# Weighted sum of gathered rows: four products of 256 columns in four column strips, and x1, y and the final norm held as feature quarter by token

## The chip, the cores and the metric

One core of a Trainium2 chip runs the program; all data is fp32. The metric is the device time of one execution in microseconds (us), lower is better.

## The reference

One layer of a decoder trunk for 1,088 tokens (1,024 of a prompt, 64 samples), model width 1,024. A mixer (projections, a recurrent group, a short convolution, attention into memory) and a layer norm give x1; after it comes PEER, a retrieval of single-neuron experts, and the second layer norm. The change lies in these last two:

```
x = LN1(alpha*x + mixer(x))                 # x1
q = x @ wq                                  # 8 heads, 2 keys each, 128 x 128 = 16384 experts
e, s = top 16 of each head                  # 128 experts a token
g = softmax(s)
act = gelu(sum_d x[t,d] * u[e[t,h,k], d])
f[t] = sum_{h,k} g[t,h,k] * act[t,h,k] * v[e[t,h,k]]
y = LN2(alpha*x + f)                        # mean and variance over the 1024 features
```

## The kernel before

The mixer runs in three blocks of tokens (384, 384, 320). PEER runs in tiles of 128 tokens (`TILES` = 8, and a ninth tile of 64), each tile in 128 **slots** (the ninth in 64), 1,088 slots in all. A slot n takes 32 tokens of the tile (a *place* `c`, four in a tile, two in the ninth), one head and a quarter `m` of the 16 experts of each token: 128 rows of the table `uv`, one on each partition, four for each of the 32 tokens. A row is 8 KB, its u half and its v half. In a slot:

- POOL (line 685) gathers the 128 rows with one indirect DMA into buffer n mod 8 of `ring`. It first waits for `used` to reach n-7, which is the weighted sum of slot n-8, the last reader of that buffer.
- PE `replicate` (L961) has spread x1 of the 32 tokens over the 128 partitions by a product with a 0/1 matrix `sel` (32 rows deep), and ACT (L1167) copied it to SBUF as `xrep`; this is done once for a group of two or four slots, 176 times in all, one group ahead.
- DVE (L1618) takes the dot product of row and `xrep`, 128x1024.
- ACT makes gelu (L1188), times the gate (L1192), and `wset` (L1197), a 128x32 matrix that holds each row's weight in its token's column.
- PE `combine(n)` (L979) multiplies `wset` with the v half and adds it up in PSUM (`ps`, two banks of 128x512, called `ybank`): two products of 512 columns. The output has 32 rows only, so each product takes a strip of 32 of the array's 128 columns. `quad(t, c)` gives the two strips: feature half 0 of place c goes to strip c, feature half 1 to strip (c+2) mod 4. It then raises `used`.

So y of a tile lies as two feature halves in the free direction, the second with its partitions turned by 64; `x1b` (x1 of the tile, later y, two buffers) lies the same way, which takes three loads (`load_x1`, L566) and three stores (`store_y`, L579) a tile on SP's queue. On DVE, `residual` (L1556, part 0 after half of a tile's slots, part 1 eight slots into the next tile) adds alpha*x1 to the sum; `finish` (L1565) takes the norm's statistics per half (`bn_stats`), swaps them between partition halves by small copies, and applies the norm; its statistics run 21 slots into the next tile (`FINISH`), in one piece between two dots. After the last slot residual and finish run at once, and SP stores the last tile.

Each engine has its own instruction stream, in an order fixed when the program is built: the slot loop, and between the slots steps of the mixer and of the queries from a plan (`PLAN`, with hand-written tables `FIRST_PE`, `FIRST_ACT`, `FIRST_DVE` for the first block), taken out by `mix(n)`. In PE's loop `replicate(g + 1)` stands before `combine(n - 1)`.

## Time and profile before

| | us |
|---|---|
| three executions | 3144.53, 3145.43, 3145.81 |
| median | 3145.43 |
| span of the profiled execution (first to last instruction) | 3140.4 |

The profiled execution's own time is not given apart from its span; the median lies 5.0 us over the span, for what is around it. The busy times of the engines in it: PE 2497.5 us, DVE 2151.5, ACT 1394.7, POOL 1208.9. The 16 DMA engines moved 1244.58 MB at a mean of 396 GB/s, 1140.92 MB of it gathered rows. In the page, a digit of a line of 40 is the busy share in tenths of a slice of 78.5 us; PEclk is the clock granted to PE, in tenths of 2.4 GHz. In a list of groups or a timeline, the bracket or the last field is the engine's idle time before the instruction, and what ended it.

### The profile page before, as it was taken

How to read it: one execution, taken by the hardware profiler on the slowest of the kernel's cores; microseconds unless marked ns; L12 is line 12 of the kernel's file. 1: busy time of each engine (PE TensorE's matmuls, PEld its weight loads, DVE VectorE, ACT ScalarE, POOL GpSimd, SP SyncE). 2: the span in 40 equal slices, each digit the busy share in tenths (PEclk: the TensorE clock that was granted, in tenths of full speed). 3: DMA queues.
4: the chain of work that ended last, by engine and by line, in shares of the span. 5: the costliest groups of instructions: out<-in, count | busy, mean ns of one | idle time of the engine just before them, and what ended most of it. 6: DMA issues, size and time to landing. Idle time of an engine off the chain costs nothing.

```text
span 3140.4 us, 36195 instructions
## 1 busy us (share of the span) xinstructions
PE 2497.5 (80%) x10228; PEld 734.3 (23%) x10228; DVE 2151.5 (69%) x4941; ACT 1394.7 (44%) x4029; POOL 1208.9 (38%) x1092
## 2 busy tenths in 40 slices
PE   8989998888886998888978879866676666666676
PEld 5633422222221332223322223311111111110010
DVE  3675778888756477887776676676667666665554
ACT  2334555555445343554544353443334444443343
POOL 0033443444444344344334334433434433443342
PEclk9999999999897998989979979977766777676766
DMA  5379999999999999999999999999999999999997
GB/s 217 132 272 416 416 417 413 383 412 420 420 420 411 420 419 417 410 404 398 419 420 415 420 409 419 420 415 419 418 409 415 421 416 412 409 415 421 419 406 317
DMA packets 188985, 1244.58 MB, mean 396 GB/s; under 512 B 21360, under 2 KB 24688, under 8 KB 48624
## 3 DMA queue, kind: packets, MB, share of 16 engines
q0 software_dynamic: 156672, 1140.92, 88.3%
q1 hardware_dynamic: 31968, 100.82, 8.4%
q8 instruction: 82, 1.34, 0.2%
q14 instruction: 119, 0.97, 0.1%
q10 hardware_dynamic: 144, 0.52, 0.1%
HBM read 1232.39 MB, written 9.79 MB: 396 GB/s over the span
## 4 chain that ended last, share of the span: by engine, by line
issue 50%; POOL 33%; PE 8%; DMA 6%; DVE 2%; ACT 1%; POOLq 0%; SPq 0%; DVEq 0%; ACTq 0%
POOL arena L685 33%; DMA arena<-in_uv,idxT 5%; PE ps L712 2%; PE ps L979 1%; PE ps L842 1%; PE ps L961 1%; POOLq L677 0%; PE ps L732 0%; DVE arena L1618 0%; PE ps L922 0%; DMA consts<-in_consts 0%; PE ps L892 0%; PE ps L748 0%; ACT wset L1197 0%; ACT wt L1192 0%
## 5 line engine op out<-in xcount | busy, mean ns | idle before, releaser
L685 POOL DMA_INDIRECT arena<-in_uv,idxT x1088 | 1208.7, 1111 | 1905.8 <-PE ps L979 1657.4
L1618 DVE CUSTOM_DVE_ANT_0 arena<-arena 128x1024 f32<-128x1024 f32 x1088 | 1328.1, 1224 | 808.1 <-DMA arena<-in_uv,idxT 726.4
L979 PE MATMUL ps<-arena,wset 128*32 128x512 f32 x4352 | 1381.7, 740 | 595.8 <-ACT wset L1197 574.4
L1188 ACT ACTIVATE gel<-acts 128x1 f32<-128x1 f32 x1088 | 219.2, 201 | 1343.1 <-DVE acts L1618 1338.2
L979 PEld LDWEIGHTS ps<-arena,wset 128*32 128x32 f32 x4352 | 173.8, 118 | 1508.7 <-ACT wset L1197 1298.4
L1197 ACT ACTIVATE wset<-arena,wt 128x32 f32<-128x32 f32 x1088 | 349.5, 321 | 36.1
L1192 ACT ACTIVATE wt<-gel,gT 128x1 f32<-128x1 f32 x1088 | 320.4, 294 | 101.7 <-ACT gel L1188 1.5
L712 PE MATMUL ps<-arena 128*128 128x384 f32 (+1 forms) x768 | 306.2, 520 | 6.6 <-DMA arena<-in_xT 6.6
L892 PE MATMUL ps<-arena 128*128 128x384 f32 (+3 forms) x896 | 287.3, 449 | 0.7 <-DVE small L1393 0.7
L961 PE MATMUL ps<-arena 32*128 32x512 f32 x704 | 238.4, 758 | 3.0 <-ACT arena L1167 2.7
L892 PEld LDWEIGHTS ps<-arena 128*128 128x128 f32 x896 | 146.6, 191 | 198.0 <-issue 154.2
L712 PEld LDWEIGHTS ps<-arena 128*128 128x128 f32 x768 | 136.3, 199 | 232.2 <-issue 182.9
L1167 ACT ACTIVATE arena<-ps 128x1024 f32<-128x1024 f32 x176 | 177.3, 1008 | 27.1 <-PE ps L961 27.0
L1188 ACT ACT_TABLE_LOAD x75 | 96.2, 1283 | 11.4 <-DVE acts L1618 10.1
L961 PEld LDWEIGHTS ps<-arena 32*128 32x128 f32 x704 | 60.8, 211 | 153.3 <-issue 139.1
L863 PE MATMUL ps<-arena 128*128 128x512 f32 x160 | 91.6, 655 | 0.0
L1618 DVE DVE_READ_ACCUMULATOR2_ANT acts<- 128x1 f32 x1088 | 89.8, 83 | 0.0
L945 PE MATMUL ps<-consts,eg 128*32 128x16 f32 x2176 | 41.3, 191 | 17.6 <-issue 17.0
L945 PEld LDWEIGHTS ps<-consts,eg 128*32 128x32 f32 x2176 | 34.4, 115 | 47.3 <-issue 46.2
L1487 DVE MAX8 val<-ps 128x8 f32<-128x128 f32 x136 | 40.1, 295 | 6.5 <-PE ps L922 5.0
L922 PE MATMUL ps<-arena 128*128 128x128 f32 x256 | 43.4, 321 | 1.0 <-ACT arena L1131 1.0
L842 PE MATMUL ps<-arena 128*128 128x512 f32 x96 | 42.3, 595 | 1.9 <-issue 1.9
(176 smaller groups left out, 1534.2 us busy)
## 6 DMA issues: line engine op xcount, KB each, us to landing
arena<-in_wq SPq DMA_DIRECT2D x56, 512.0 KB
arena<-in_w_in SPq DMA_DIRECT2D x47, 512.0 KB
arena<-in_uv,idxT POOLq DMA_INDIRECT x1088
arena<-in_w_outs SPq DMA_DIRECT2D x24, 512.0 KB, 8.5
scratch_x<-arena SPq DMA_DIRECT2D x9, 512.0 KB
arena<-in_ln SPq DMA_DIRECT2D x4, 1024.0 KB, 13.5
arena<-in_xT SPq DMA_DIRECT2D x4, 768.0 KB, 18.8
arena<-scratch_x SPq DMA_DIRECT2D x18, 128.0 KB
```

What stands on the lines that cost most here:

```text
L685: pool.indirect_dma_start(out=ring[n % RING], out_offset=None, in_=A["uv"], in_offset=bass.IndirectOffsetOnAxis(ap=idxT[t % 2][:, col:col ...
L712: last = mm(out_, w_[:, kk, :], x_[:, kk, :], start=kk == 0, stop=kk == KD - 1)
L863: last = mm(bank[MB[ti]], y_, w_[:, k2, :], start=k == 0, stop=k == KD - 1)
L892: last = mm(o_[:, 0:hi - lo], w_[:, k, :], x8(zone2, b)[:, k, lo:hi], start=k == 0, stop=k == KD - 1)
L945: last = mm(kbank[32 * jj:32 * jj + 32, o:o + 16].rearrange("p (c m) -> p c m", c=4), eg[:, e0 + 16 - 16 * e:e0 + 48 - 16 * e], pick[:, 2 ...
L961: last = mm(xr[:, hf * HALF:(hf + 1) * HALF], sel_s[lo:lo + 32, m_, :], x1b[t % 2][lo:lo + 32, from_:from_ + HALF], start=True, stop=True)
L979: last = mm(ps[r0:r0 + 32, hf * HALF:(hf + 1) * HALF], wset[n % SETS][:, :], v[:, hf * HALF:(hf + 1) * HALF], start=first, stop=final)
L1167: A_(xrep[g % 2], xr, ACT.Copy).then_inc(xr_cp, 1)
L1188: A_(gel[:, n % COLS:n % COLS + 1], acts[:, n % COLS:n % COLS + 1], ACT.Gelu).then_inc(gelus, 1)
L1192: A_(wt[:, n % COLS:n % COLS + 1], gel[:, n % COLS:n % COLS + 1], ACT.Copy, scale=gT[t % 2][:, col:col + 1]).then_inc(weights, 1)
L1197: A_(wset[n % SETS][:, :], masks[:, m_, :], ACT.Copy, scale=wt[:, n % COLS:n % COLS + 1]).then_inc(sets, 1)
L1618: V.tensor_tensor_reduce(out=ring[n % RING][:, 0:D], in0=ring[n % RING][:, 0:D], in1=xrep[g % 2], scale=1.0, scalar=0.0, op0=ALU.mult, op1 ...
```

## The change

`place(t, c)` takes the stead of `quad`. The features are in four quarters of 256: quarter q has partitions (and strip) 32q to 32q+31, and place c has columns 256c to 256c+255. `combine` is four products of 256 columns, one for each strip. `x1b` lies the same way, so that `replicate` is four products of 256 columns from four row groups; it is split in two parts, one before and one after `combine(n - 1)`. Loads of x1 and stores of y are four DMAs of 32 partitions, in pieces of 1 KB. The second norm's weights are loaded as quarters (`ln2q`, 0.25 MB instead of 1 MB, and no later second load). The statistics are taken for each place, and passed between four partition groups by 16 copies.

```diff
@@ SP
-            sp.dma_start(x1b[t % 2][:, 0:HALF], O["x1"][r0:r0 + P, 0:HALF]).then_inc(ld_x1b[t % 2], 16)
-            sp.dma_start(x1b[t % 2][0:HP, HALF:], O["x1"][r0 + HP:r0 + P, HALF:]).then_inc(ld_x1b[t % 2], 16)
-            sp.dma_start(x1b[t % 2][HP:P, HALF:], O["x1"][r0:r0 + HP, HALF:]).then_inc(ld_x1b[t % 2], 16)
+            for q in range(4):
+                sp.dma_start(quarter(x1b[t % 2], t, q), by_quarter(O["x1"], t, q)).then_inc(ld_x1b[t % 2], 16)
...
-                load("ln2", ln2, A["ln"][2:4].partition_broadcast(P))
+                for q in range(4):
+                    load("ln2", ln2q[32 * q:32 * q + 32], A["ln"][2:4, q * QUART:(q + 1) * QUART].partition_broadcast(32))
@@ PE
-        def replicate(g):
+        def replicate(g, part):
...
-            for hf in range(2):
-                lo = 32 * quad(t, c_)[hf]
-                from_ = hf * HALF if t < TILES else 0
-                last = mm(xr[:, hf * HALF:(hf + 1) * HALF], sel_s[lo:lo + 32, m_, :],
-                          x1b[t % 2][lo:lo + 32, from_:from_ + HALF], start=True, stop=True)
-            last.then_inc(xr_mm, 1)
+            x0 = place(t, c_) * QUART
+            for q in (part, 2 + part):
+                last = mm(xr[:, q * QUART:(q + 1) * QUART], sel_s[32 * q:32 * q + 32, m_, :],
+                          x1b[t % 2][32 * q:32 * q + 32, x0:x0 + QUART], start=True, stop=True)
+            last.then_inc((xr_half, xr_mm)[part], 1)
...
-            for hf in range(2):
-                r0 = 32 * quad(t, c_)[hf]
-                last = mm(ps[r0:r0 + 32, hf * HALF:(hf + 1) * HALF], wset[n % SETS][:, :],
-                          v[:, hf * HALF:(hf + 1) * HALF], start=first, stop=final)
+            y0 = place(t, c_) * QUART
+            for q in range(4):
+                last = mm(ps[32 * q:32 * q + 32, y0:y0 + QUART], wset[n % SETS][:, :],
+                          v[:, q * QUART:(q + 1) * QUART], start=first, stop=final)
...
-                replicate(g + 1)
+                replicate(g + 1, 0)
...
                 combine(n - 1)
+            if ahead:
+                replicate(g + 1, 1)
@@ DVE, residual and finish
-            for hf in range(2):
-                lo = HP * (hf ^ part)
...
-                did(V.scalar_tensor_tensor(yo, yo, ALPHA, ybank[lo:lo + HP, hf * HALF:(hf + 1) * HALF], ALU.mult,
-                                           ALU.add))
+            yo = x1b[t % 2][:, part * HALF:(part + 1) * HALF]
+            did(V.scalar_tensor_tensor(yo, yo, ALPHA, ybank[:, part * HALF:(part + 1) * HALF], ALU.mult, ALU.add))
...
-            did(V.tensor_copy(bsr[:, 0:6], bst[:, 0:6]))
-            did(V.tensor_copy(bsr[0:HP, 6:12], other[HP:P, :]))
-            did(V.tensor_copy(bsr[HP:P, 6:12], other[0:HP, :]))
+            for q in range(4):
+                for to in range(4):
+                    did(V.tensor_copy(bsr4[32 * to:32 * to + 32, 0:n_, q, :], bst4[32 * q:32 * q + 32, 0:n_, :]))
```

PE issues 7,716 products after instead of 5,188, DVE 4,491 instructions instead of 4,331, SP 244 DMAs instead of 222; ACT and POOL issue the same number.

PE in the opening of PEER, while the first block's output projection (L842, after the change L835) still runs between slots (L961/L958 is `replicate`, L979/L976 `combine`, L945/L940 the selection of indices). Before:

```order
L842 MATMUL ps<-arena 128x512 x8
L961 MATMUL ps<-arena 128x512 x2
L979 MATMUL ps<-arena,wset 32x512 x4
L945 MATMUL ps<-consts,eg 32x16 x32
L961 MATMUL ps<-arena 128x512 x2
L979 MATMUL ps<-arena,wset 32x512 x4
L842 MATMUL ps<-arena 128x512 x8
```

And now:

```order
L835 MATMUL ps<-arena 128x512 x8
L958 MATMUL ps<-arena 128x256 x2
L976 MATMUL ps<-arena,wset 32x256 x4
L958 MATMUL ps<-arena 128x256 x2
L976 MATMUL ps<-arena,wset 32x256 x4
L940 MATMUL ps<-consts,eg 32x16 x32
L958 MATMUL ps<-arena 128x256 x2
L976 MATMUL ps<-arena,wset 32x256 x4
L958 MATMUL ps<-arena 128x256 x2
L976 MATMUL ps<-arena,wset 32x256 x4
L835 MATMUL ps<-arena 128x512 x8
```

Where two combines stood together behind one replicate, each now stands behind one half of it; nothing else has moved.

DVE after the last dot of the program (residual, statistics, norm of the ninth tile). Before:

```order
L1562 SCALAR_TENSOR_TENSOR arena<-arena,ps 64x512 x2
L1574 BN_STATS bst<-arena 128x6
L1577 COPY bsr<-bst 128x6
L1578 COPY bsr<-bst 64x6
L1579 COPY bsr<-bst 64x6
L1581 BN_AGGR mv<-bsr 128x2
L1585 RECIPROCAL mv<-mv 128x1
L1595 SCALAR_TENSOR_TENSOR arena<-arena,mv 128x512
L1601 SCALAR_TENSOR_TENSOR arena<-arena,mv 128x512
```

And now:

```order
L1563 SCALAR_TENSOR_TENSOR arena<-arena,ps 128x512
L1574 BN_STATS bst<-arena 128x6 x2
L1578 COPY bsr<-bst 32x2x6 x16
L1581 BN_AGGR mv<-bsr 128x2 x2
L1586 RECIPROCAL mv<-mv 128x4
L1591 SCALAR_TENSOR_TENSOR arena<-arena,mv 128x256 x2
L1595 SCALAR_TENSOR_TENSOR arena<-arena,mv 128x256 x2
```

Three copies have become 16; the adds are one instruction for two, and the norm's two passes are in two pieces each.

## Rows read from the trace of the kernel before

**Rows 1.** The page, part 3: queue and kind: packets, MB, share of 16 engines.

```profile
q0 software_dynamic: 156672, 1140.92, 88.3%
...
q8 instruction: 82, 1.34, 0.2%
```

**Rows 2.** The page, part 5: instruction, count | busy us, mean ns | idle before, releaser.

```profile
L685 POOL DMA_INDIRECT arena<-in_uv,idxT x1088 | 1208.7, 1111 | 1905.8 <-PE ps L979 1657.4
L1618 DVE CUSTOM_DVE_ANT_0 arena<-arena 128x1024 f32<-128x1024 f32 x1088 | 1328.1, 1224 | 808.1 <-DMA arena<-in_uv,idxT 726.4
L979 PE MATMUL ps<-arena,wset 128*32 128x512 f32 x4352 | 1381.7, 740 | 595.8 <-ACT wset L1197 574.4
```

**Rows 3.** Stretches: PE, PEld, DVE, ACT, POOL busy us (count), PEclk, DMA share, GB/s.

```profile
200.00:210.00 10.00, 9.58 (x94) 4.23 (x94) 4.94 (x12) 2.74 (x8) 1.83 (x2) 1.00 0.75 313
620.00:630.00 10.00, 8.46 (x91) 3.24 (x91) 8.21 (x19) 6.11 (x16) 3.52 (x3) 0.98 0.81 292
250.00:1900.00 1650.00, 1402.83 (x6107) 446.83 (x6105) 1214.01 (x2880) 799.58 (x2244) 685.05 (x591) 0.92 1.01 413
1900.00:3110.00 1210.00, 855.59 (x3140) 164.76 (x3138) 772.06 (x1677) 490.54 (x1557) 489.34 (x471) 0.75 1.01 416
```

**Rows 4.** DMA, 3112 to 3141 us: GB/s in 40 slices of 0.72 us.

```profile
GB/s 418 429 418 429 418 418 407 418 429 418 395 136 57 23 34 34 23 34 23 23 34 11 0 0 0 0 0 0 0 0 0 0 0 0 0 0 178 184 0 0
```

**Rows 5.** Timeline, the DVE near the end: start us, us, instruction, idle before.

```profile
3115.01 1.23 DVE L1618 CUSTOM_DVE_ANT_0 arena<-arena 128x1024 f32<-128x1024 f32 x1 [0.89 <-DMA arena<-in_uv,idxT]
...
3118.47 1.23 DVE L1618 CUSTOM_DVE_ANT_0 arena<-arena 128x1024 f32<-128x1024 f32 x1 [2.23 <-DMA arena<-in_uv,idxT]
```

**Rows 6.** DMA, 3114 to 3119 us: packets by queue.

```profile
q14 instruction: 1, 0.01, 0.4%
```

**Rows 7.** DMA, 2966 to 2977 us: packets by queue.

```profile
q8 instruction: 1, 0.02, 0.6%
```

**Rows 8.** Timeline, the DVE in the same stretch.

```profile
2971.30 1.22 DVE L1618 CUSTOM_DVE_ANT_0 arena<-arena 128x1024 f32<-128x1024 f32 x1 [1.25 <-DMA arena<-in_uv,idxT]
...
2973.76 1.23 DVE L1618 CUSTOM_DVE_ANT_0 arena<-arena 128x1024 f32<-128x1024 f32 x1 [1.24 <-DMA arena<-in_uv,idxT]
```

**Rows 9.** Timeline, PE at 198 to 209 and at 3123 us.

```profile
198.50 1.05 PE L979 MATMUL ps<-arena,wset 128*32 128x512 f32 x4 [2.52 <-ACT wset L1197]
...
206.54 1.13 PE L961 MATMUL ps<-arena 32*128 32x512 f32 x4
207.60 1.07 PE L979 MATMUL ps<-arena,wset 128*32 128x512 f32 x8
...
3123.29 1.92 PE L979 MATMUL ps<-arena,wset 128*32 128x512 f32 x4 [1.50 <-ACT wset L1197]
```

**Rows 10.** Timeline, POOL at 209 us.

```profile
208.94 1.87 POOL L685 DMA_INDIRECT arena<-in_uv,idxT  x1 [8.17 <-PE ps L979]
```

**Rows 11.** DMA, 1206 to 1216 us, while packets of 1,280 B load: by queue.

```profile
q1 hardware_dynamic: 478, 0.59, 16.7%
```

**Rows 12.** Timeline, the tail.

```profile
3113.42 1.51 POOL L685 DMA_INDIRECT arena<-in_uv,idxT  x1 [2.92 <-PE ps L979]
...
3128.34 1.23 DVE L1618 CUSTOM_DVE_ANT_0 arena<-arena 128x1024 f32<-128x1024 f32 x1 [1.22 <-DMA arena<-in_uv,idxT]
...
3130.60 1.05 PE L979 MATMUL ps<-arena,wset 128*32 128x512 f32 x4 [0.90 <-ACT wset L1197]
3131.70 1.40 DVE L1562 SCALAR_TENSOR_TENSOR arena<-arena,ps 64x512 f32<-64x512 f32 x2 [2.13 <-PE ps L979]
3133.24 0.69 DVE L1574 BATCH_NORM_STATS2 bst<-arena 128x6 f32<-128x512 f32 x1
3133.97 0.17 DVE L1577 COPY bsr<-bst 128x6 f32<-128x6 f32 x1
3134.18 0.17 DVE L1578 COPY bsr<-bst 64x6 f32<-64x6 f32 x1
...
3137.02 1.14 SPq L588 DMA_DIRECT2D out_y<-arena  x2
```

More of the change, by code:

```diff
@@ L28 @@
 HALF = D // 2
+QUART = D // 4
 WIN = 3
@@ L455, in build @@
     gath = [sem(f"gath{i}") for i in range(RING)]
-    xr_mm, xr_cp, dots, gelus, weights, sets, used, res_done = (
-        sem("xr_mm"), sem("xr_cp"), sem("dots"), sem("gelus"), sem("weights"), sem("sets"), sem("used"),
+    xr_mm, xr_half, xr_cp, dots, gelus, weights, sets, used, res_done = (
+        sem("xr_mm"), sem("xr_half"), sem("xr_cp"), sem("dots"), sem("gelus"), sem("weights"), sem("sets"), sem("used"),
         sem("res_done"))
@@ L514, in last_query, with place, by_quarter, quarter @@
         return "wq", (SIDES // 2 if b == 0 else SIDES) - 1
-    def quad(t, c):
-        return (c if t < TILES else c % 2), ((c + 2) % 4 if t < TILES else c % 2 + 2)
+    def place(t, c):
+        return c if t < TILES else c % 2
+    def by_quarter(dram, t, q):
+        n_ = 4 if t < TILES else 2
+        return dram[t * P:t * P + 32 * n_, q * QUART:(q + 1) * QUART].rearrange("(c r) f -> r c f", c=n_)
+    def quarter(buf, t, q):
+        n_ = 4 if t < TILES else 2
+        return buf[32 * q:32 * q + 32, 0:n_ * QUART].rearrange("r (c f) -> r c f", c=n_)
     def per(u):
@@ L903, in run @@
                 after(pe, "act", 0, "xe", (0, 1))
-                replicate(0)
+                replicate(0, 0)
+                yield
+                replicate(0, 1)
                 yield
@@ L969, in combine @@
             quads = 4 if t < TILES else 2
-            first = m_ == 0 and h == 0 and c_ < quads
-            final = m_ == 3 and h == (7 if t < TILES else 3) and c_ >= 4 - quads
+            first = m_ == 0 and h == 0 and c_ in (0, 2)[:quads // 2]
+            final = m_ == 3 and h == (7 if t < TILES else 3) and c_ in (1, 3)[2 - quads // 2:]
             if t and n == TILE_END[t - 1]:
@@ L989, in _ @@
             g, i = SLOT[n][4:6]
-            if i == 0 and g + 1 < len(GROUPS_OF):
-                replicate(g + 1)
+            ahead = i == 0 and g + 1 < len(GROUPS_OF)
+            if ahead:
+                replicate(g + 1, 0)
             if n in AT:
@@ L1001, in _ @@
                 combine(n - 1)
+            if ahead:
+                replicate(g + 1, 1)
             mix(n)
@@ L1567, in finish @@
         def finish(t):
+            n_ = 4 if t < TILES else 2
             residual(t, 1 if t < TILES else 0)
             yield
-            halves = [(0, mv), (1, mvr)] if t < TILES else [(0, mv)]
-            yout = x1b[t % 2]
-            for hf, _ in halves:
-                did(V.bn_stats(bst[:, hf * 6:(hf + 1) * 6], yout[:, hf * HALF:(hf + 1) * HALF]))
+            z = [x1b[t % 2][:, c * QUART:(c + 1) * QUART] for c in range(n_)]
+            for c in range(n_):
+                did(V.bn_stats(bst4[:, c, :], z[c]))
             chain.wait()
-            other = bst[:, 6:12] if t < TILES else bst[:, 0:6]
-            did(V.tensor_copy(bsr[:, 0:6], bst[:, 0:6]))
-            did(V.tensor_copy(bsr[0:HP, 6:12], other[HP:P, :]))
-            did(V.tensor_copy(bsr[HP:P, 6:12], other[0:HP, :]))
+            for q in range(4):
+                for to in range(4):
+                    did(V.tensor_copy(bsr4[32 * to:32 * to + 32, 0:n_, q, :], bst4[32 * q:32 * q + 32, 0:n_, :]))
             chain.wait()
-            link(V.bn_aggr(mv[:, 0:2], bsr[:, :]))
+            for c in range(n_):
+                did(V.bn_aggr(mv4[:, c, 0:2], bsr4[:, c].rearrange("p q k -> p (q k)")))
+            chain.wait()
             dve.nop().then_inc(v2_done, 1)
@@ L1584, in finish @@
             dve.wait_ge(sd2_done, t + 1)
[L1585 to L1596 removed]
+            link(V.reciprocal(mv4[:, :, 3], mv4[:, :, 2]))
+            yield
+            if t == 0:
+                dve.wait_ge(ld["ln2"], 64)
+            for c in range(n_):
+                did(V.scalar_tensor_tensor(z[c], z[c], mv4[:, c, 0:1], ln2q[:, 0, :], ALU.subtract, ALU.mult))
             yield
             chain.wait()
[L1599 to L1602 removed]
+            for c in range(n_):
+                did(V.scalar_tensor_tensor(z[c], z[c], mv4[:, c, 3:4], ln2q[:, 1, :], ALU.mult, ALU.add))
             chain.wait()
```

68 lines of the change are left out of this document (20 added, 48 removed).

## Prediction, made before the changed kernel was run

> **What bounds the kernel now.** I read the page's list of queues first. The queue q0 carries the gathers: 139,264 rows of 8 KB (1,088 x 128) and 1,141 MB, and takes 88.3% of 16 engines' time [rows 1]. The reader is to see that one kind of transfer fills the DMA engines. The costliest groups say the same from the other side [rows 2]: the gathers' instructions take 1,208.7 us of POOL, the dots wait 726 of their 808 idle us for DMA, and the combines wait for ACT's `wset`, which itself hangs on the dot. The stretches show it in time: DMA share 1.01 at 413 and 416 GB/s from 250 to 3110 us, with PE busy 1,403 of 1,650 us and then 856 of 1,210 [rows 3]. A slot moves 128 x 8,192 B = 1.049 MB, at about 421 GB/s 2.49 us; the dots stand 2.46 us apart [rows 8]. POOL's waits for PE's `used` are the ring's bookkeeping: the last gather is issued at 3113.42 and its dot runs at 3128.34, 14.9 us or six slots later [rows 12], so five slots of gathers stand in the queue.
>
> A finer reading decides the small terms. At the end the rate is 395 or more up to about 3120 us, and then 23 to 34 GB/s for some 7 us [rows 4]: 1/16 of 421 is 26. One DMA engine of the sixteen is 7 us behind, and the end waits for it. 
> **The change part by part.** *The combine.* It takes 1.05 us at full clock (two passes over 512 columns) and 1.92 at half. Two combines of different places ran their 8 matmuls together in 1.07 us at 207.60 [rows 9]: four strips work at once, so four strips of 256 columns should take half of 1.05 and some start, 0.62. That is -0.43 us of PE in each of 1,088 slots, 468 us of PE at full clock. Nearly all lies beside the DMA stream: worth nothing while the share of DMA is 1.01 [rows 3]. Two places are left, the opening and the tail.
>
> *The opening.* At 208.94 POOL has waited 8.17 us for `used` [rows 10], behind a batch of PE's output projection (199.5 to 206.5). In front of that batch stands one combine at 198.50 (1.05 us), behind it a replicate (1.13) and the pair at 207.60 [rows 9]. The combine ahead saves 0.43. Behind the batch the order shows half a replicate (0.56), one combine (0.62), half a replicate, one combine: 2.36 us for the 2.13 of before. The pair already used four strips and saves nothing, but its first `used` comes 0.5 us sooner. I take -1.0 us for this wait and its like at 221. Bounds: 0 and -2.3 (both waits in full, 2 x (0.43 + 0.56), and 0.3 for the split).
>
> *Replicate split.* Four products of 256 instead of two of 512 have the same columns, two at a time; the switch from replicate to combine shows as at most 0.07 us (206.54 + 1.13 against 207.60) [rows 9]. It is now made 176 times more, beside DMA: 0.
>
> *At 620 to 630 us* the DMA share is 0.81 and PE busy 8.46 of 10 [rows 3]: a place without cover. There four combines save 1.7 us of PE, and the first tile's statistics, 3.5 us longer (below), hold the dots up. I take 0; bounds -1.7 and +3.5.
>
> *DVE's statistics*, eight times in the stream: bn_stats in four of 256 for two of 512 (0.69 each [rows 12]; about the same), 16 copies for 3 at 0.20 apart (3133.97 and 3134.18 [rows 12]: +2.6), aggregates 4 for 1 (+0.6), together +3.5 with gaps. Five queued slots, some 11 us, cover it: 0 after the first tile. Without that cover it would be +3.5 a tile.
>
> *Fetches.* DVE +160 instructions, 1.25 blocks of 128, each 0.97 on the late engine [rows 5, 6]: +1.2; bounds 0 and 2. PE +2,528 products, each four instructions (two weight loads, two passes): +10,112, at 16 KB for 256 another 40 blocks over the 82 [rows 1]: 0, since rows 8 lose nothing; if all fell on the late engine, 40 x 0.97 = +39.
>
> *Small pieces.* x1 and y now move in 8,704 pieces of 1 KB for 4,352 of 2 KB. While 1,280 B packets load, 478 of them take 16.7% of 160 us, 56 ns each [rows 11]; an 8 KB row takes 88.3% x 50,246 us / 139,264 = 319 ns [rows 1]. The line through both gives about 46 ns for 1 KB and 85 for 2 KB, so +7 for a split, 4,352 x 7 / 16 = +2.0 us. The norm's weights lose 1.05 MB, 2.5 us. Sum -0.5; bounds -2.5 (pieces free) and +20 (a 1 KB piece as slow as 2 KB, which the 56 ns speak against).
>
> *The tail*, from the last combine to the end, has no cover [rows 12]: combine -0.43; residual one add of 128x512 (0.7) for two taking 1.40, -0.7; bn_stats two of 256 for 0.69, +0.1; 13 more copies at 0.20, +2.6; one more aggregate +0.15; norm in halves +0.25; four stores for two, which took 1.14 to issue, +1.05. Sum +3.0; bounds +2 and +4.5.
>
> **The sum.** -1.0 + 0 + 0 + 1.2 - 0.5 + 3.0 = +2.7. The profiled execution's span is 3140.4, and the median 3145.43 lies 5.0 over it for what is around; the change alters nothing there. So 3143.1 of span and **3148.1 us**. The bounds of the terms give 3141 to 3157.
>
> **The rivals.** *Faster, the opening is shortened by every combine* (3138.9): PE's saving pulls the gathers ahead in every slot from 198 to 235 us (15 slots of 2.49, -6.4), the two halved replicates with them (-1.1), at 620 (-1.7), and the tail comes at its lower bound (-1.0): 2.7 + 1.0 - 6.4 - 1.1 - 1.7 - 1.0 = -6.5. For it: DMA has gaps there [rows 3, 10]. Against: pairs had four strips already.
>
> *Slower, half clock* (3165): the granted clock is 0.92 where PE is busy 85% and 0.75 where 71% [rows 3]. From 250 to 1900 us PE's work for a slot is 0.85 x 2.49 = 2.1 us, now 1.7. If the clock falls as it does later, 1.7 / 0.66 = 2.57 us exceeds the slot of 2.49. It decides from a granted clock under 1.7 / 2.49 = 0.68 in that stretch; at 0.66 in all 660 slots it costs 55 us, in a third of them 18. Against: work that takes longer makes PE busier, and the ring covers short waits. The Trainium skill, "TensorE: Matmul & The Clock Gate", Part 1, says that the throttled clock is the default and activity releases it; by that rule the shortened combine buys itself a slower clock, and the trace agrees in direction (0.92 against 0.75).
>
> *Slower, the statistics starve the gathers* (3160): a piece 3.5 us longer holds the dots, these hold `used`, and POOL issues late. It decides when what the piece adds to the lateness already there exceeds 11 us; where the cover is half gone, 8 x 1.5 = +12.
>
> *Slower, PE's fetches* (3187): 40 x 0.97 on the late engine. Against: rows 8. The Trainium skill, "Runtime: NRT & Kernel Launch", section "Instruction fetch mechanics", calls the crossing of a 16 KiB block mostly hidden; 1.34 MB / 82 blocks agrees in size [rows 1].
>
> *The four products don't run at once* (3149): a combine then takes 1.05 or more, the tail and the opening lose 0.43 each; for it nothing, against it the pair at 207.60 [rows 9]. The time would hardly tell; the combine's mean would.
>
> **How the numbers follow.** 0.2%, about what a measurement of this kernel can tell from no change, is 6.3 us: 3139.1 to 3151.7. The forecast 0.64, of it 0.10 above 3151.7 (its terms' upper bounds); the opening 0.14, of it 0.08 below 3139.1; half clock 0.07; statistics 0.09; fetches 0.02; products not at once 0.04. Faster 0.08; slower 0.10 + 0.07 + 0.09 + 0.02 = 0.28; within 0.64. The forecast's own range is 3142 to 3155. For 8 in 10 I go down to 3139, leaving out 0.08, and up to 3160, leaving out half clock, fetches and a third of the statistics, 0.12.
>
> **What would show it.** Right: combine's mean from 740 ns (two passes in a row counted) to about 0.62 us from first to last at full clock; PE's busy time about 400 us less, less than 468 by a lower clock; dots still 2.49 apart in the middle with DMA share 1.01; from the last combine to the end 3.0 us more; one engine's lag of some 7 us again. Wrong: a DMA share under 1 between 250 and 3110, a granted clock under 0.68 before 1900 us, gaps in the gathers 21 slots into a tile, dots 3.4 apart around fetches of q8, or 1 KB packets over 60 ns.

## The result, and the profile after

| | before | after |
|---|---|---|
| median of the executions, us | 3144.98 (3144.28 to 3145.81, 4 runs) | 3161.14 (3158.04 to 3163.27, 4 runs) |
| span of the profiled execution | 3140.4 | 3157.2 |
| mean granted clock of TensorE | 0.858 | 0.731 |

The ratio is 1.0051 with a 95% interval of 1.0039 to 1.0063: the change makes the kernel 12 to 20 us slower, where 3148.1 was forecast with a range up to 3160.0. A second set of five executions (after_again below) gave 3160.15 us beside 3143.64, ratio 1.0056 (1.0042 to 1.0069).

The clock line of the page before, then from the page after the busy times, the same line and the queues of instruction fetches, and its groups around the combine and the replicate:

```profile
PEclk9999999999897998989979979977766777676766
```

```profile
PE 2243.1 (71%) x15284; PEld 875.8 (28%) x15284; DVE 2165.7 (69%) x5101; ACT 1397.5 (44%) x4029; POOL 1238.7 (39%) x1092
...
PEclk9987988889896998878868869955555555555555
...
q8 instruction: 121, 1.98, 0.3%
q14 instruction: 120, 0.98, 0.1%
```

```profile
L678 POOL DMA_INDIRECT arena<-in_uv,idxT x1088 | 1238.4, 1138 | 1888.5 <-PE ps L976 1639.7
L1611 DVE CUSTOM_DVE_ANT_0 arena<-arena 128x1024 f32<-128x1024 f32 x1088 | 1326.5, 1223 | 821.5 <-DMA arena<-in_uv,idxT 665.8
L976 PE MATMUL ps<-arena,wset 128*32 128x256 f32 x8704 | 955.6, 524 | 863.3 <-ACT wset L1198 842.6
...
L958 PE MATMUL ps<-arena 32*128 32x256 f32 x1408 | 337.1, 565 | 6.3 <-ACT arena L1167 6.1
```

The combine did get shorter, 524 ns a pass of 256 columns for 740 ns a pass of 512 [rows 2], and PE as a whole is busy 254 us less. The replicate is a different matter: its passes took 238.4 us of PE before and take 337.1 now. PE's fetches rose from 82 blocks to 121, near the 40 that were forecast. And the clock line has fallen: it stands at 5, half speed, from the 27th slice on, where it had stood at 6 and 7. The same stretches as in [rows 3]:

```profile
250.00:1900.00 1650.00, 1276.09 (x8847) 519.53 (x8845) 1221.70 (x2953) 803.09 (x2244) 710.15 (x590) 0.83 1.01 411
1900.00:3110.00 1210.00, 722.33 (x5290) 224.83 (x5286) 778.14 (x1748) 489.80 (x1553) 495.75 (x468) 0.57 1.01 415
```

DMA is as busy as before, and its rate is 0.2 to 0.5% lower (411 for 413 GB/s, 415 for 416), which over these 2,860 us is some 11 us by the rounded rates. So the middle of the kernel is bound by DMA as forecast, and the loss must be sought at the places where the rate falls.

I took the start of each dot in both profiled executions and subtracted; the difference is called the dot's lateness from here on. Dot 0 starts 1.1 us later, dot 4 1.4, dot 10 9.3, dot 140 6.3, dot 170 10.0, dot 400 9.9, dot 880 16.2, dot 1060 14.2, the last 14.2; behind it the end takes 2.6 us more: 16.8 together. (The first 1.1 lie ahead of the first dot, in the mixer, which the change doesn't touch.) The places are the opening (+7.9 from dot 4 to 10, of which 3 are back by dot 140), the stretch of the first tile's statistics (+3.7, dots 140 to 170), some 6 us in steps behind later tiles, a gain of 1.8 behind the eighth tile, and the tail.

**The opening.** The timeline of PE before has the two batches of the output projection, 16 passes each, at 7.13 us:

```profile
199.48 7.13 PE L842 MATMUL ps<-arena 128*128 128x512 f32 x16
...
212.06 7.13 PE L842 MATMUL ps<-arena 128*128 128x512 f32 x16
```

After:

```profile
196.72 0.70 PE L958 MATMUL ps<-arena 32*128 32x256 f32 x4
199.94 1.08 PE L976 MATMUL ps<-arena,wset 128*32 128x256 f32 x8 [2.53 <-ACT wset L1198]
200.95 9.43 PE L835 MATMUL ps<-arena 128*128 128x512 f32 x16
...
218.55 9.17 PE L835 MATMUL ps<-arena 128*128 128x512 f32 x16
```

PE waits 2.53 us for `wset` ahead of the combine at 199.94, as it waited 2.52 before [rows 9]. Before, the combine behind the wait still ran at full clock (1.05 us). Now it takes 1.08, which is half clock for this form (0.64 elsewhere), and the batch behind it 9.43; the second takes 9.17. That is 4.3 us for the two batches. A further 1.0 us lies between them, where the selection's short products (L945, now L940) take 2.35 us for 1.36: PE then stands twice for about 0.45 us with nothing to wait for in the profile, where it stood once. Both batches sit on the path: the dots behind them wait for the copy of `xrep`. The dots 4, 6 and 10 before, and after:

```profile
201.43 1.23 DVE L1618 CUSTOM_DVE_ANT_0 arena<-arena 128x1024 f32<-128x1024 f32 x1
...
208.77 1.23 DVE L1618 CUSTOM_DVE_ANT_0 arena<-arena 128x1024 f32<-128x1024 f32 x1 [4.96 <-ACT arena L1167]
...
221.35 1.23 DVE L1618 CUSTOM_DVE_ANT_0 arena<-arena 128x1024 f32<-128x1024 f32 x1 [4.88 <-ACT arena L1167]
```

```profile
202.87 1.23 DVE L1611 CUSTOM_DVE_ANT_0 arena<-arena 128x1024 f32<-128x1024 f32 x1
...
213.32 1.22 DVE L1611 CUSTOM_DVE_ANT_0 arena<-arena 128x1024 f32<-128x1024 f32 x1 [8.06 <-ACT arena L1167]
...
230.65 1.23 DVE L1611 CUSTOM_DVE_ANT_0 arena<-arena 128x1024 f32<-128x1024 f32 x1 [7.64 <-ACT arena L1167]
```

**The first tile's statistics.** Timeline of DVE and of POOL after, and the stretch of 12 us behind (columns as in [rows 3]):

```profile
628.69 0.07 DVE L1611 DVE_READ_ACCUMULATOR2_ANT acts<- 128x1 f32 x1
...
630.11 3.32 DVE L1578 COPY bsr<-bst 32x24 f32<-32x24 f32 x16
633.47 0.63 DVE L1581 BATCH_NORM_AGGREGATE mv<-bsr 128x2 f32<-128x24 f32 x4
...
635.49 1.23 DVE L1611 CUSTOM_DVE_ANT_0 arena<-arena 128x1024 f32<-128x1024 f32 x1 [0.26 <-DVE arena L1403]
```

```profile
634.18 0.94 POOL L678 DMA_INDIRECT arena<-in_uv,idxT  x1 [3.36 <-PE ps L976]
639.14 0.94 POOL L678 DMA_INDIRECT arena<-in_uv,idxT  x1 [4.03 <-PE ps L976]
643.38 0.95 POOL L678 DMA_INDIRECT arena<-in_uv,idxT  x1 [3.31 <-PE ps L976]
```

```profile
642.00:654.00 12.00, 11.85 (x62) 4.60 (x62) 9.76 (x21) 4.80 (x16) 3.95 (x4) 0.69 0.88 302
```

The 16 copies take 3.32 us, the piece from 628.69 to 634.1 lies between two dots, POOL waits 3 to 4 us three times, and DMA falls to 302 GB/s. Before, the same stretch moved 426, but the kernel before has a hole as well, 20 us earlier: 351 GB/s from 620 to 642 us, where it is 404 after. So the two are compared over the whole neighbourhood, before and then after:

```profile
560.00:700.00 140.00, 119.86 (x472) 37.55 (x470) 122.51 (x295) 79.16 (x213) 61.81 (x52) 0.95 0.99 402
620.00:642.00 22.00, 19.65 (x136) 6.95 (x135) 18.52 (x41) 14.12 (x36) 8.38 (x8) 0.99 0.91 351
```

```profile
560.00:700.00 140.00, 108.24 (x758) 43.96 (x758) 120.56 (x304) 77.05 (x207) 60.97 (x51) 0.87 0.99 390
620.00:642.00 22.00, 13.95 (x137) 5.76 (x137) 18.22 (x55) 14.43 (x35) 7.15 (x7) 0.81 1.00 404
```

390 for 402 GB/s over 140 us is 4.2 us of transfer, which agrees with the 3.7 that the dots lose.

**The tail**, to be read beside [rows 12]:

```profile
3142.59 1.23 DVE L1611 CUSTOM_DVE_ANT_0 arena<-arena 128x1024 f32<-128x1024 f32 x1 [1.23 <-DMA arena<-in_uv,idxT]
...
3144.86 1.08 PE L976 MATMUL ps<-arena,wset 128*32 128x256 f32 x8 [1.38 <-ACT wset L1198]
3146.01 0.69 DVE L1563 SCALAR_TENSOR_TENSOR arena<-arena,ps 128x512 f32<-128x512 f32 x1 [2.18 <-PE ps L976]
3146.84 0.75 DVE L1574 BATCH_NORM_STATS2 bst<-arena 128x6 f32<-128x256 f32 x2
3147.62 3.10 DVE L1578 COPY bsr<-bst 32x12 f32<-32x12 f32 x16
3150.76 0.38 DVE L1581 BATCH_NORM_AGGREGATE mv<-bsr 128x2 f32<-128x24 f32 x2
...
3153.67 1.75 SPq L584 DMA_DIRECT2D out_y<-arena  x4
```

The last combine gains nothing (1.08 for 1.05), since it runs at half clock where the one before ran at full. (The full clock there is chance of the profiled execution: in those of before_halved and before_16, further down, the same combine took 1.92 us.) The copies take 3.10 us for 0.57, the residual add 0.69 for 1.40, and the four stores 1.75 for 1.14.

### The profile page after: what moved, and what is told of

It reads as the page before. It is cut to its first block, busy times and chain, and to the rows that moved or that the text cites. A ratio compares the mean times of both kernels' runs of the same rounds, so it can differ in the third digit from the quotient of the medians.

```text
span 3157.2 us, 46488 instructions
## 1 busy us (share of the span) xinstructions
PE 2243.1 (71%) x15284; PEld 875.8 (28%) x15284; DVE 2165.7 (69%) x5101; ACT 1397.5 (44%) x4029; POOL 1238.7 (39%) x1092
## 4 chain that ended last, share of the span: by engine, by line
issue 54%; POOL 36%; PE 5%; DMA 2%; DVE 1%; POOLq 1%; ACT 0%; SPq 0%; DVEq 0%; ACTq 0%
POOL arena L678 36%; PE ps L705 2%; DMA arena<-in_uv,idxT 2%; PE ps L835 1%; POOLq L670 1%; PE ps L725 0%; DMA consts<-in_consts 0%; PE ps L885 0%; PE ps L741 0%; DVE arena L1611 0%; DVE arena L1436 0%; PE ps L750 0%; PE ps L769 0%; SPq L554 0%; DVE bsr L1578 0%
## 5 line engine op out<-in xcount | busy, mean ns | idle before, releaser
L678 POOL DMA_INDIRECT arena<-in_uv,idxT x1088 | 1238.4, 1138 | 1888.5 <-PE ps L976 1639.7
L976 PE MATMUL ps<-arena,wset 128*32 128x256 f32 x8704 | 955.6, 524 | 863.3 <-ACT wset L1198 842.6
L976 PEld LDWEIGHTS ps<-arena,wset 128*32 128x32 f32 x8704 | 200.1, 126 | 1549.6 <-ACT wset L1198 1403.1
L705 PE MATMUL ps<-arena 128*128 128x384 f32 (+1 forms) x768 | 339.0, 566 | 7.4 <-DMA arena<-in_xT 7.1
L958 PE MATMUL ps<-arena 32*128 32x256 f32 x1408 | 337.1, 565 | 6.3 <-ACT arena L1167 6.1
L885 PE MATMUL ps<-arena 128*128 128x384 f32 (+3 forms) x896 | 303.4, 469 | 0.7 <-DVE small L1394 0.7
L958 PEld LDWEIGHTS ps<-arena 32*128 32x128 f32 x1408 | 141.3, 245 | 222.7 <-issue 207.4
L705 PEld LDWEIGHTS ps<-arena 128*128 128x128 f32 x768 | 148.4, 217 | 158.2 <-issue 112.7
L885 PEld LDWEIGHTS ps<-arena 128*128 128x128 f32 x896 | 154.0, 200 | 123.7 <-issue 81.2
L856 PE MATMUL ps<-arena 128*128 128x512 f32 x160 | 98.2, 698 | 0.0
L940 PE MATMUL ps<-consts,eg 128*32 128x16 f32 x2176 | 40.7, 199 | 14.8 <-issue 14.5
L835 PE MATMUL ps<-arena 128*128 128x512 f32 x96 | 46.6, 644 | 1.9 <-issue 1.9
L940 PEld LDWEIGHTS ps<-consts,eg 128*32 128x32 f32 x2176 | 35.9, 130 | 35.2 <-issue 34.3
L917 PEld LDWEIGHTS ps<-arena 128*128 128x128 f32 x256 | 40.0, 238 | 14.5 <-issue 11.8
```

Of the source, the lines that this page charges most:

```text
L678: pool.indirect_dma_start(out=ring[n % RING], out_offset=None, in_=A["uv"], in_offset=bass.IndirectOffsetOnAxis(ap=idxT[t % 2][:, col:col ...
L705: last = mm(out_, w_[:, kk, :], x_[:, kk, :], start=kk == 0, stop=kk == KD - 1)
L856: last = mm(bank[MB[ti]], y_, w_[:, k2, :], start=k == 0, stop=k == KD - 1)
L885: last = mm(o_[:, 0:hi - lo], w_[:, k, :], x8(zone2, b)[:, k, lo:hi], start=k == 0, stop=k == KD - 1)
L917: last = mm(scores[u][:, si * NK:(si + 1) * NK], q_of(t, k)[:, si * P:(si + 1) * P], keysT[:, a_:a_ + NK], start=True, stop=True)
L958: last = mm(xr[:, q * QUART:(q + 1) * QUART], sel_s[32 * q:32 * q + 32, m_, :], x1b[t % 2][32 * q:32 * q + 32, x0:x0 + QUART], start=True, ...
```

## The experiments

Each ran beside the kernel before on the same chip; times are medians, and the ratio is to the kernel before, with its 95% interval. The kernel before came out at 3143.99, 3145.66, 3143.64 and 3144.37 us in the four sets.

**Extra work for PE.** Each doubled combine has four more products with zero weights (`zw`); fill_all is without the bound on n:

```diff
+            if not first and n < 32:
+                for q in range(4):
+                    mm(ps[32 * q:32 * q + 32, y0:y0 + QUART], zw[:, :], v[:, q * QUART:(q + 1) * QUART], start=False,
+                       stop=False)
```

> Every combine of the first 32 slots but those that open a bank is doubled by four products with zero weights, so that PE works there as long as before the change (about 1.2 us a combine); the sums stay the same. Clock theory (PE idles more in the opening, its clock falls to half, and the output projection's batches of 16 take 9.2 to 9.4 us for 7.13): the batches at about 200 and 212 to 218 us are back at 7.1 to 7.5 us, the gathers waiting for them come 4 us sooner, and the time is 3161 - 4 to 6 = 3155 to 3157. Order theory (the second half of replicate stands behind a combine and its copy comes late): the filler makes it later still, the time is 3161 to 3165. Statistics, fetches, small pieces: 3161, unchanged.

3165.18 us, ratio 1.0065 (1.0051 to 1.0079): slower than the change, or level. The first batch stayed at 8.83 us (8.93 in after_again). The filler stood behind the wait for `wset`, so that the wait ahead of the batch remained (2.10 us for 2.53); it only made PE's queue longer. So this run decides nothing about the clock.

> The same filler in every slot, 1,088 slots but the few that open a bank. Clock theory: granted clock from 0.73 back to 0.85 or more, PE busy about 2500 us, time 3152 to 3156 if the half clock also costs the steps after 250 us, 3155 to 3157 if it costs only in the opening. Fetch theory (PE's blocks of 256 instructions cost on the late DMA engine): 4,300 x 4 products more, 17,000 instructions or so counting weight loads (x2), 68 to 136 blocks more, +10 us or more over fill_open. Statistics and small pieces: as fill_open.

3175.87 us, ratio 1.0107 (1.0091 to 1.0122). Clock and busy time are near those of the kernel before (0.865 and 2547 us for 0.858 and 2498), and the time is some 32 us over it:

```profile
PE 2546.8 (80%) x23852; PEld 1132.2 (36%) x23852; DVE 2166.1 (68%) x5102; ACT 1397.8 (44%) x4029; POOL 1224.9 (39%) x1092
...
PEclk9998999999897999989979979977777777777777
```

With the clock back over most of the kernel it is slowest, so a clock bought by work on PE's queue doesn't pay. The first batch still took 8.83 us, and most of the loss lies in the opening: 18.1 us of lateness from dot 4 to dot 140, for 4.9 in the change. From dot 140 to the last dot it is 10.8, for 7.9 in the change, so that the clock that came back there gained nothing that shows. The run doesn't separate the queue on PE from the 67 blocks more that PE fetches (188 for 121); the next one bears on it.

**The number of products alone**, on the kernel before:

```diff
-            for hf in range(2):
-                r0 = 32 * quad(t, c_)[hf]
+            for k in (0, 2, 1, 3):
+                r0 = 32 * quad(t, c_)[k // 2]
+                last = mm(ps[r0:r0 + 32, k * 256:(k + 1) * 256], wset[n % SETS][:, :],
+                          v[:, k * 256:(k + 1) * 256], start=first and k % 2 == 0, stop=final and k % 2 == 1)
```

(replicate likewise)

> The kernel before, with combine and replicate as four products of 256 columns in the same two strips or row groups: PE has the changed kernel's 7,716 products and 39 to 40 more instruction blocks, but the same busy time and clock as before. Fetch theory: 3145 + 6 to 39. Clock, order, statistics, pieces: 3145 to 3146, the granted clock 0.86.

3143.11 us, ratio 0.9996 (0.9987 to 1.0005). The page:

```profile
PE 2498.3 (80%) x15284; PEld 1110.8 (35%) x15284; DVE 2152.3 (69%) x4941; ACT 1396.0 (44%) x4029; POOL 1219.9 (39%) x1092
...
PEclk9999999999897998999979979967777776676766
...
q8 instruction: 121, 1.98, 0.3%
```

39 blocks more are fetched, as in the changed kernel, and nothing is lost; the interval leaves room for 1.6 us. The fetch rival falls. PE has the change's number of products here, and the same wait, but combines of 1.06 us, and the batch behind the wait stays at full clock:

```profile
201.64 1.06 PE L979 MATMUL ps<-arena,wset 128*32 128x256 f32 x8 [2.51 <-ACT wset L1197]
202.63 7.13 PE L842 MATMUL ps<-arena 128*128 128x512 f32 x16
```

The replicate in four products together takes 1.13 us as with two; it is the change's two parts that take 0.70 each.

**Fewer copies.** This version leaves out the exchange between the partition groups, so that its y is not the layer's:

```diff
-                for to in range(4):
-                    did(V.tensor_copy(bsr4[32 * to:32 * to + 32, 0:n_, q, :], bst4[32 * q:32 * q + 32, 0:n_, :]))
+                did(V.tensor_copy(bsr4[:, 0:n_, q, :], bst4[:, 0:n_, :]))
```

> The statistics' 16 copies of 32 partitions are 4 copies of 128 partitions; the norm then uses the mean and variance of a quarter of the features in each partition group (that part of the computation is changed). Statistics theory: the tail is 12 x 0.2 = 2.4 us shorter and the step of +2.8 us behind the first tile's statistics (620 to 650 us) goes, as do the steps of 1 to 2 us behind some later tiles: 3161 - 2.4 - 2.8 - 2 = 3154. Clock and order theory: only the tail changes, 3158.7, with the steps as they are.

3150.99 us, ratio 1.0023 (1.0014 to 1.0032): 9 to 10 us gained, more than any theory gave. The tail is 2.7 us shorter, and the copies got not only fewer but closer together. Four copies of 128 partitions take 0.42 us, where 16 of 32 take 3.32:

```profile
631.13 0.42 DVE L1577 COPY bsr<-bst 128x24 f32<-128x24 f32 x4
```

Its opening lost 6.8 us from dot 4 to dot 10, where the change lost 7.9, so that little of the gain comes from there. Then with the statistics passed between all four groups again, in six copies:

```diff
-                did(V.bn_stats(bst4[:, c, :], z[c]))
+                did(V.bn_stats(bsr4[:, c, 0, :], z[c]))
             chain.wait()
-            for q in range(4):
-                for to in range(4):
-                    did(V.tensor_copy(bsr4[32 * to:32 * to + 32, 0:n_, q, :], bst4[32 * q:32 * q + 32, 0:n_, :]))
+            for lo, to in ((0, 64), (64, 0)):
+                did(V.tensor_copy(bsr4[to:to + 64, 0:n_, 1, :], bsr4[lo:lo + 64, 0:n_, 0, :]))
+            chain.wait()
+            for q in range(4):
+                to = 32 * (q ^ 1)
+                did(V.tensor_copy(bsr4[to:to + 32, 0:n_, 2:4, :], bsr4[32 * q:32 * q + 32, 0:n_, 0:2, :]))
```

> bn_stats writes its result in place, two copies of 64 partitions and then four of 32 with two quarters each spread the statistics: 6 copies for 16, the result is the same. Statistics theory, from four_copies (12 fewer copies, -10.2 us, 2.4 of it in the tail): 10 fewer and one more wait for DVE's own results, 3161 - 7 to 9 = 3152 to 3154. Rival (four_copies came out faster by chance of the opening): 3161 - 2 = 3159.

3153.89 us, ratio 1.0020 (1.0011 to 1.0030): the statistics theory's number, with a tail 1.9 us shorter than the change's. Where the rest is gained is read off all profiles together, further down.

**The order of replicate.** Both parts before the combine:

```diff
                 replicate(g + 1, 0)
+                replicate(g + 1, 1)
...
-            if ahead:
-                replicate(g + 1, 1)
```

> Both parts of replicate stand before the combine, as in the kernel before; all else as in the changed kernel. Order theory (the second part behind the combine makes xrep late in the opening, where dots wait 8 us for ACT's copy): the opening's +8 us falls by 3 or more, time 3161 - 3 to 8 = 3153 to 3158, and the dot behind the first batch starts by 211 instead of 213.3. Clock theory: the batches still take 9 us, time 3159 to 3162.

3158.24 us, ratio 1.0033 (1.0021 to 1.0045), 2 to 3 us under the change by the medians, with intervals that overlap. The batches still take 9.37 and 8.45 us, and dot 10 is 8.0 us later against dot 4 (7.9 in the change), so the order isn't what the opening loses. (The second part still waits for the first to end: the two together take 1.47 us, for 1.13 before.)

```profile
200.61 9.37 PE L835 MATMUL ps<-arena 128*128 128x512 f32 x16
...
219.53 8.45 PE L835 MATMUL ps<-arena 128*128 128x512 f32 x16
```

**Filler in the wait itself.** fill_first has the table {2: 4, 3: 1, 4: 2} instead:

```diff
+            for _ in range({2: 4, 5: 1, 6: 1}.get(n, 0)):
+                for q in range(4):
+                    mm(ps[32 * q:32 * q + 32, 0:QUART], zw[:, :], sel_s.rearrange("p m q -> p (m q)")[:, 0:QUART],
+                       start=False, stop=False)
             pe.wait_ge(sets, n + 1)
```

> Products with zero weights fill PE's wait of 2.5 us before the combine ahead of the first batch (four rounds of four products, about 2.4 us), and one round stands before each of the two combines ahead of the second batch; the sums stay the same. Clock theory: the first batch takes 7.1 to 7.5 us for 9.4, the second 7.1 to 8, time 3161 - 2 to 4.5 = 3156.5 to 3159, and the stream behind starts earlier by that. Rival (what the opening loses is order and not the clock): time 3161 to 3163.

3154.25 us, ratio 1.0029 (1.0019 to 1.0038). PE (L968 is filler, L836 the projection):

```profile
196.81 1.93 PE L968 MATMUL ps<-arena,zw 128*32 128x256 f32 x32
...
199.97 7.13 PE L836 MATMUL ps<-arena 128*128 128x512 f32 x16
...
217.69 7.51 PE L836 MATMUL ps<-arena 128*128 128x512 f32 x16
```

With the wait of 2.53 us filled but for 0.66, the first batch is back at 7.13 us. The second took 7.51; the replicate that starts at 211.65, behind the selection's short products, is already at half clock (1.22 us for 0.70), ahead of the rounds meant to hold it. From dot 4 to dot 10 the dots still lose 5.9 us, since the rounds stand on the path too.

> As fill_wait, but the filler is four rounds in the wait ahead of the first batch, one round before the first combine behind it and two before the second (0.5 us each, behind the batch where the clock was still full), none ahead of the second batch. Clock theory: clock stays full from 207 to 217 us, the second batch takes 7.1 us for 9.2, and the loss of the opening against the kernel before is 3 to 4 us for 8; time 3161 - 4 to 6 = 3155 to 3157. Rival (the rounds themselves delay the gathers as much as the clock gives back): as fill_wait, 3154 to 3158, with the second batch at 7.5 or more.

3156.78 us, ratio 1.0039 (1.0025 to 1.0052).

```profile
202.82 7.13 PE L836 MATMUL ps<-arena 128*128 128x512 f32 x16
...
217.18 7.13 PE L836 MATMUL ps<-arena 128*128 128x512 f32 x16
```

Now both batches take 7.13 us, and the dots lose 2.2 us from dot 4 to dot 10; the same filler gives 2.1 to 2.2 in the three combined kernels below, and all kernels of the new layout without filler lose 6.8 to 8.0. So it is shown that the half clock of the batches comes from PE's idling. The filler brings back some 6 us there: 4.3 are the two batches, about 1.0 is the selection, which takes 1.31 us again with the rounds ahead of it, the rest small products at half clock. What it is worth at the end is less certain. In the profiled executions the last dot's lateness against dot 4 is 12.1 us here and 12.8 and 12.3 in the two profiles of the change, but this one was the slowest of its five (3160.57, median 3156.78). The medians of fill_wait and fill_first are 3 to 7 us under the change's, with intervals that partly overlap.

**Pieces of 1 KB**, on the kernel before (x1's loads; the stores likewise):

```diff
-            sp.dma_start(x1b[t % 2][:, 0:HALF], O["x1"][r0:r0 + P, 0:HALF]).then_inc(ld_x1b[t % 2], 16)
+            for k in range(4):
+                hf, a_, b_ = k // 2, k * 256, k * 256 + 256
...
+                elif hf == 0:
+                    sp.dma_start(x1b[t % 2][:, a_:b_], O["x1"][r0:r0 + P, a_:b_]).then_inc(ld_x1b[t % 2], 16)
```

> The kernel before with x1 and y moved in pieces of 1 KB, six DMAs a tile instead of three and four stores instead of two at the end. Pieces theory (the changed kernel lost 1.1 us behind each of the tiles from the third to the sixth): 3144 + 1.1 in the tail (two more issues of 0.57) + 5 to 9 in the stream = 3150 to 3154. Prediction's term (+2.0 for the splits): 3144 + 1.1 + 2.0 = 3147.

3150.04 us, ratio 1.0012 (1.0003 to 1.0021), so +1 to +7 us, which leaves both theories standing. The trace shows a second cost beside the packets. The x1 loads of the second tile stand in SP's queue ahead of the weights `wq`; three more of them put those back, and PE waits:

```profile
277.67 1.00 PE L896 MATMUL ps<-arena 128*128 128x384 f32 x2 [2.27 <-DMA arena<-in_wq]
```

The dots lose 4.4 us there (dots 20 to 40), 2.4 more from dot 50 to the last, and the tail 1.0. But this version issues six loads a tile, the change four. In the change the loads of x1 and of the norm's weights do put `wq` back by 2.6 us in SP's queue, and PE isn't seen to wait for it. So of this run only the 2.4 and some of the tail carry over to the change.

**Copies alone**, on the kernel before:

```diff
+            for k in range(13):
+                did(V.tensor_copy(extra[32:64, k * 6:k * 6 + 6], bst[32:64, 0:6]))
```

> The kernel before with 13 more copies of 32x6 in each tile's statistics, into a tile that nothing reads, so that it issues 16. Statistics theory: 2.6 in the tail and what the stream loses, most of it behind the first tile: 3145 + 2.6 + 2 to 5 = 3150 to 3153. If the stream's cover holds in the kernel before, whose dots are less late: 3145 + 2.6 + 0.8 (104 more instructions to fetch) = 3148.

3146.99 us, ratio 1.0010 (1.0000 to 1.0019). The trace shows that this run doesn't add what it was built to add. All its copies read and write the same 32 partitions, and then they stand 0.07 us apart, 1.05 us in all:

```profile
625.99 1.05 DVE L1582 COPY extra<-bst 32x6 f32<-32x6 f32 x13
```

The change's copies go from one partition group to the next and stand 0.20 us apart, each starting only when the one before has ended. So the piece between the dots grew by 1.1 us here, where the change's grew by 3.3, and the tail's by 1.0 (0.9 more of the tail is the last combine at half clock). The dot behind the first tile's piece is 1.0 us later, all that was added, and nothing of it is left at the last dot. Whether the kernel before would cover 3.3 us is not tried by any run.

**The change once more, and both mends.**

> The changed kernel once more, beside the next three on one chip, since its executions spread more (3158.0 to 3163.3) than those of the kernel before. All theories: 3158 to 3163.

3160.15 us, ratio 1.0056 (1.0042 to 1.0069).

> six_copies and fill_first together. If the clock in the opening and the statistics are separate costs, their gains add: 3161 - 7 - 5 = 3149, still above the kernel before (3144 to 3146) by the small pieces, the tail's stores and what the opening keeps. If the gathers' cover lets one hide the other: 3152 to 3154.

3149.12 us, ratio 1.0023 (1.0014 to 1.0032). By the median the gains add; by the ratio it is level with six_copies (1.0020). So the filler's gain at the end isn't shown beyond the spread of the runs.

**The statistics in shorter pieces**, all 16 copies kept:

```diff
-            elif t >= 1 and n - TILE_END[t - 1] >= FINISH:
+            elif t >= 1 and n - TILE_END[t - 1] >= FINISH - 3:
...
+                if q in (1, 3):
+                    yield
```

> The changed kernel with all 16 copies, but the statistics taken in four pieces over four slots: bn_stats three slots earlier, eight copies in the slot behind, eight in the next, the aggregates where they were. DVE issues the same instructions and the tail is the same. Lateness theory (a piece of 5.5 us in one slot holds the dots, they hold the ring's buffers, and the gathers stop): 3160.5 - 5 to 7 = 3154 to 3156, and behind the first tile's statistics DMA stays above 400 GB/s where it fell to 300. Rival (what costs is the amount, more instructions for DVE to fetch and to work off): 3159 to 3162.

3158.11 us, ratio 1.0044 (1.0030 to 1.0058): 2 us under the change's second set, less than the 5 to 7 expected, with overlapping intervals. Behind the first tile DMA moves 377 GB/s from 642 to 654 us for 302; but rep_first, with all 16 copies in one piece, has 372 there. That one stretch varies too much between profiles to weigh the copies by.

The whole stream does it better. This is the lateness that each profile gains from dot 140 to the last dot, us:

| statistics | profiles | lateness gained |
|---|---|---|
| 16 copies, one piece | after, after_again, rep_first, fill_wait, fill_first, fill_open, fill_all | 7.9, 6.8, 7.9, 6.3, 9.7, 7.2, 10.8 |
| 16 copies, four slots | spread16 | 3.8 |
| 6 copies | six_copies, combo, combo2, combo3 (the last in three slots) | 2.0, 2.1, 4.3, 2.4 |
| 4 copies | four_copies | 1.4 |
| kernel before, with one edit | before_1k, before_16, before_halved | 3.1, -0.3, -4.0 |

The 16 copies in one piece and the six or four don't overlap: the mean of the first group is 8.1, of the others 2.4. So the long piece of copies costs about 5 us in the stream, an estimate, since the last row tells how far single profiles of the kernel before differ. How much of it goes with the length of the piece and how much with the number of copies stays open: spread16 gains 3 to 4 us by this table, but its profiled execution was the fastest of its five (3154.69), and by the medians it gains 2.

**Clock and queue behind the opening** (more filler from the 10th to the 16th combine, the second tile's x1 and the norm's weights 40 slots later), and the same with the six copies' statistics in three slots:

```diff
-            if n == 20:
+            if n == 60:
                 after(sp, "pe", 0, "op", (2, 1))
```

> combo, with filler also from the 10th to the 16th combine (three rounds behind the 10th, two before the 11th, one before each of the next five), and with the loads of the second tile's x1 and of the norm's weights issued 40 slots later. In combo the dots lost 2.1 us up to slot 20 and 7 more by slot 30, half of it for good, with PE at half clock from 229 us. Clock and queue theory: PE's clock is full from 229 to 280 us, the loss by slot 100 falls from 4.4 to 2 or less, time 3149 - 2 to 3 = 3146 to 3147. Rival (that loss comes from elsewhere): 3148.5 to 3150.

3151.80 us, ratio 1.0023 (1.0013 to 1.0033): not under combo, so the forecast of this run failed.

> combo2, with the six copies' statistics taken in three slots. If what combo2 still loses behind tiles is lateness of dots: 1 to 2 us below combo2, 3144 to 3146, level with the kernel before. If it is the small pieces and the tail: as combo2.

3149.04 us, ratio 1.0014 (1.0005 to 1.0023): under combo2 by 3 us, with overlapping intervals, and not level with the kernel before. In combo2's profile the clock behind the opening is only partly back, 0.66 and 0.83 in the stretches from 240 to 260 and from 260 to 280 us, for 0.50 and 0.65 after the change. Dot 60 is 1.8 us earlier against dot 4 than in the kernel before, and 10 dots later, when the moved loads run, 6 us are lost again. No version of the new layout came level with the kernel before; combo3, the best by its ratio, is 1.6 to 7 us over it.

## Why the prediction was wrong

- *What bounds the kernel*: right. From 250 to 3110 us DMA's share is 1.01 and PE's 254 us saved are worth nothing there.
- *The combine*: the mechanism and the size were right at full clock (0.64 for a forecast of 0.62), and no more than that: at half clock it takes 1.08, and the mean is 524 ns a pass. Its group is busy 426 us less, near the forecast of about 400 for the whole of PE.
- *Replicate split*, 0: half a replicate was put at 0.56 us and takes 0.70, since the second part waits for the first; both together in rep_first take 1.47 for 1.13. The switch from replicate to combine isn't the cause, since rep_first has no more of them than before_halved, where four products take 1.13. With the lower clock the replicates are busy 99 us more. That and other groups at half clock leave 254 of the 426.
- *The opening*, -1.0 with bounds 0 and -2.3: **this step failed, in sign.** It measured +7.9 from dot 4 to dot 10, some 5 of it still there at dot 140. I reckoned with PE's work there at full clock, because the trace of before shows 1.00. Behind the shorter combines (0.64 us for 1.05) the clock fell to 1.2 GHz in a wait as long as before (2.53 us for 2.52), and two batches of 7.13 us took 9.43 and 9.17. I had half clock as a rival, but placed it between 250 and 1900 us; there the clock did fall (0.83) and DMA covered it. The Trainium skill, "TensorE: Matmul & The Clock Gate", Part 1, names the throttled clock as the default that activity releases. The runs with filler agree, since filling the wait alone brought the batch back to 7.13.
- *620 to 630 us and the statistics*, 0 with a bound of +3.5 and 0 for later tiles: the second failed step. The versions with six or four copies are 6 to 10 us faster by the medians, 1.9 to 2.7 of it in the tail, and gain about 5 us less lateness in the stream. The cover of 11 us was read at the end of the kernel, where the dots wait for DMA. Behind the first tile they wait for DVE's own work: the dot at 635.49 stands behind L1403, and its rows were asked for 22.8 us earlier, at 612.72, for 14.9 at the end. The kernel before showed as much (292 GB/s from 620 to 630 us [rows 3]), and I called the place one without cover and still took 0. Why the later tiles lose as well, with DMA's share at 1.01, no run shows.
- *Fetches*: PE's 0 was right (before_halved), DVE's +1.2 too small to be seen.
- *Small pieces*, -0.5, of it +2.0 for the splits: not refuted. before_1k gives +1 to +7, of which 4.4 us in its profile come from more issues in SP's queue than the change has, and 2.4 fit the splits. The term left out SP's queue. The kernels of the new layout gain 1.5 to 3.3 us behind the eighth tile (dots 1040 to 1060; 1.8 in the change), where the second load of the norm's weights is gone, and the versions of the kernel before between -0.6 and 0.6; that the missing load is the cause is likely, not shown.
- *The tail*, +3.0: measured +2.6; the combine's -0.43 was not had, and the stores took 0.61 us more for a forecast of 1.05.
- *The rivals*: the statistics (3160) came nearest, by their mechanism and partly by their size, and had a chance of 0.09. Half clock (3165, 0.07) had the right cause in the wrong place: in the stream DMA's share stayed at 1.01, and the clock told in the opening. That 3160 lies so near 3161 is in part luck; the statistics alone don't give it.
- *The range and the base*: the bounds of the terms don't add up to the 3157 given. With the +20 for the pieces they come to 3175, and with -0.5 for them to 3155. And the 5.0 us between span and median are not all around the program: the four executions of the change take 1.8 to 1.9 us more than their spans, so the profiled one before took about 3142.2 us, some 3 under its median. The forecast time is not changed by that.

Open is how the steps of about 1 us behind the third to sixth tile divide between copies and pieces, how much of the opening's loss reaches the end, and what the 5 us are that combo and combo3 keep over the kernel before, of which the tail has 0.7.

## What to carry to other kernels

An engine with a clock that follows its activity must be costed at both levels wherever the change takes work from it, above all ahead of a long batch that is on the path; a wait of 2.5 us behind shorter combines was enough here. Where many small copies between partition groups replace a few, count them and cut their number first: doubling what each carries took 16 to 6. A cover read in one stretch holds for that stretch only. And a run that is to add a known amount must be read in its own trace before its time is used: the 13 copies meant to add 2.6 us added 1.05.
